# A hybrid decoder layer: weight slot views that start 8, 16 or 24 bytes further in or further back

## The chip, the core and the metric

The kernel runs on one core of one Trainium2 chip. The metric is the device time of one execution in microseconds (us), median of three runs.

## What is computed

One decoder layer over 256 tokens of width 1024, all in float32. The reference, cut to its products:

```python
h = rms_norm(x, attn_norm)
q_r, k_r, v_r, g_r, q_m, k_m, v_m = split(h @ w_in)        # 1024 x 6144
y_ret  = (group_norm(retention(rotary(q_r), rotary(k_r), v_r)) * silu(g_r)) @ w_ret_o
y_moba = attention(rms_norm(q_m), rms_norm(k_m), v_m) @ w_moba_o
gate_ret, gate_moba = split(sigmoid(h @ w_gate + b_gate))  # 1024 x 2048
x = x + (gate_ret * y_ret + gate_moba * y_moba) @ w_out
h = rms_norm(x, ffn_norm)
u_gate, u_val = split(causal_conv(h @ w_up))               # 1024 x 5632
x = x + (silu(u_gate) * u_val) @ w_down                    # 2816 x 1024
```

## The kernel before, in words

The weights are cut into 77 halves of 128 x 2048 float32 (1 MB each), numbered n = 0 to 76, and pass through four slots; half n uses slot r = n mod 4. A half is loaded by DMA into `w_raw{r}`. Then it is split in two: ScalarE (ACT) writes its high part, rounded to float32r, to the first 2048 elements of a view of `w_pair{r}` (line 635), and VectorE (DVE) writes the remainder, the low part, to the 2048 elements behind (line 912). Every product x @ w is three matmuls: high by high, high by low, low by high. The activations are split the same way, in `h_hi`, `h_lo`, `a_hi` and `a_lo`.

TensorE (PE) uses a half in one of two roles. A matmul has a stationary operand, 128 columns that are loaded before it (a weight load, PEld), and a moving operand that streams through.

- In **channel halves** the weights are the stationary operand and the activations move, 256 columns a matmul (`channel_half`, lines 377 to 379): 48 matmuls a half. There are 44 such halves: Q_R, K_R, G_R0, G_R1, GATE_R0, GATE_R1, RET_O0, RET_O1, GATE_M0, GATE_M1, MOBA_O0 and MOBA_O1 (n = 4 to 11 and 24 to 39), and n = 46 to 65 of the up-projection. Each slot has 11 of them.
- In **token halves** the activations are stationary and the weights move, 512 columns a matmul: 24 matmuls a half. These are V_R0, V_R1 (n = 0 to 3), Q_M0 to V_M1 (n = 12 to 23), all in `token_half`, lines 342 to 344; OUT0, OUT1 and UP0 (n = 40 to 45, `one_tile`, lines 530 to 532); and the down-projection (n = 66 to 76, lines 612 to 615). Without the down-projection these are 22 halves, five each in slots 2 and 3 and six each in slots 0 and 1.

`w_parts(n, r)` gives the two views of a slot. A slot is `SHIFT + 2 * HALF_ELEMS` elements long, `SHIFT` is 8 elements (32 bytes), so 32 bytes are spare. A view for moving weights starts 32 bytes in and a view for stationary weights at 0. The halves n = 66 and 67 (slots 2 and 3) are split inside a hardware loop whose views are those of stationary weights, so they start at 0 although their weights move.

Tensors stand one behind the other in SBUF, each rounded up to 32 bytes. In the built program `w_pair0` to `w_pair3` begin at bytes 110976, 127616, 144256 and 160896 of a partition, all multiples of 128; `h_hi`, `h_lo`, `a_hi` and `a_lo` begin at 49312, 57504, 65696 and 88224, all 32 past a multiple of 64.

ACT and DVE split half n as soon as half n - 4 has been used (`half_used`) and its data are there (`raw_loaded`); PE waits for `lo_ready` of the half that it begins. Between splits ACT and DVE read PSUM banks and do norms, softmax, gates and the convolution. The same engines also write and read `u_in`, rows of 258 elements whose data begin at the third element.

Of the kernel before, what the change touches and what calls it, by code (L numbers as in the profile page):

```python
# [20 lines left out]
SHIFT = 8  # L21
# [34 lines left out]
def hybrid_layer(nc, x, x_chan0, x_chan1, x_chan2, weights, gain_row_in, cols, ident_in, mask_in, rotary_in, decay_in, out):  # L56
# [8 lines left out]
    with ExitStack() as ctx:  # L65
# [154 lines left out]
        def w_parts(n, r=None):  # L220

            r = n % SLOTS if r is None else r
            if isinstance(n, int):
                moving = n // 2 in TOKEN_BLOCKS or n >= DOWN_FIRST_HALF + 2
            else:
                moving = False
            first = SHIFT if moving else 0
            return [w_pair[r][:, first + HALF_ELEMS * i:first + HALF_ELEMS * i + HALF_ELEMS] for i in range(2)]

        block = ctx.enter_context(nc.Block())  # L230
# [89 lines left out]
        def _(pe):  # L320
# [12 lines left out]
            def token_half(out_banks, n, tiles, first, last, before=None, src=(h_hi, h_lo)):  # L333

                hi, lo = (w.rearrange("p (k c) -> p k c", k=4) for w in w_parts(n))
                for kk, t in [(kk, t) for kk in range(4) for t in range(NT)]:
                    if before and t == 0:
                        before(kk)
                    k = tiles[kk]
                    s_hi, s_lo = (part[:, k, P * t:P * t + P] for part in src)  # L340
                    o = out_banks[t][:, :]
                    mm(o, s_hi, hi[:, kk, :], start=(first and kk == 0), stop=False)  # L342
                    mm(o, s_hi, lo[:, kk, :], start=False, stop=False)  # L343
                    ins = mm(o, s_lo, hi[:, kk, :], start=False, stop=(last and kk == 3))  # L344
                return ins
# [22 lines left out]
            def channel_half(banks, n, slot, r_hi, r_lo, h):  # L368

                hi, lo = (w.rearrange("p (k c) -> p k c", k=4) for w in w_parts(n, slot))  # L370
                for m in range(4):
                    o = banks[m // 2][:, SEQ * (m % 2):SEQ * (m % 2) + SEQ]
                    for kk in range(4):
                        k = 4 * h + kk
                        s_hi, s_lo = hi[:, kk, P * m:P * m + P], lo[:, kk, P * m:P * m + P]

                        mm(o, s_hi, r_hi[:, k, :], start=(k == 0 and m % 2 == 0), stop=False)  # L377
                        mm(o, s_hi, r_lo[:, k, :], start=False, stop=False)  # L378
                        ins = mm(o, s_lo, r_hi[:, k, :], start=False, stop=(k == KT - 1 and m % 2 == 1))  # L379
                return ins  # L380
# [23 lines left out]

            pe.wait_ge(zeros_ready, 1)
            zeros = w_parts(SLOTS - 1)[1][:, 0:512]
            def keep_warm(count):
                for _ in range(count):
# [895 lines left out]
```

## Time and profile before

| | |
|---|---|
| median of 3 runs | 471.55 us (471.36 to 471.68) |
| the profiled execution | 471.34 us, span 469.5 us |
| granted TensorE clock | 0.999 of full |
| PE, PEld, DVE, ACT busy | 99%, 91%, 64%, 54% of the span |
| weight halves through the slots | 77, of which 44 stationary, 33 moving |

The busy time of PE says that it always had a matmul under way. Matmuls overlap in such a profile, so their mean durations add up to more than the span; how fast they follow each other is read from the starts of two halves and the number of matmuls between them.

### The profile page before, as it was taken

The page shows a single profiled execution, that of the slowest core. Times are in us where ns is not written, and L with a number is a line of the kernel's source. Part 1 is how long each engine was busy: PE and PEld are TensorE (multiplying, and loading weights), DVE is VectorE, ACT ScalarE, POOL GpSimd, SP SyncE. Part 2 cuts the span into 40 slices and gives each one's busy share as a digit, 9 for nine tenths or more (in the row PEclk, how much of TensorE's full clock was granted, in tenths as well). Part 3 has the DMA queues.
Part 4 walks back from the last instruction along what each step waited for, and adds up shares of the span by engine and source line. Part 5 has one row for each costly group of instructions (what it writes and reads, how often), then busy time and mean ns, then how long its engine had stood idle before and what let it go on. Part 6 is the DMA issues. An engine that isn't in the chain of part 4 may idle for free.

```text
span 469.5 us, 7781 instructions
## 1 busy us (share of the span) xinstructions
PE 463.6 (99%) x3117; PEld 426.8 (91%) x3117; DVE 300.1 (64%) x364; ACT 254.5 (54%) x362; POOL 19.6 (4%) x27
## 2 busy tenths in 40 slices
PE   8999999999999999999999999999999999999997
PEld 5889999888888999999999788999999999988885
DVE  4797883764665547355338676688778888884312
ACT  5775432147774839334445355777777767663400
POOL 0210000311110001000000000000000000000000
PEclk9999999999999999999999999999999999999999
DMA  7997444254445523843453633616555555548002
GB/s 273 423 403 271 180 179 181 91 179 154 147 151 211 223 102 136 357 157 131 167 188 135 269 136 131 241 69 238 202 187 197 193 207 193 188 139 309 0 1 89
DMA packets 13978, 87.20 MB, mean 186 GB/s; under 512 B 1536, under 2 KB 1920, under 8 KB 4352
## 3 DMA queue, kind: packets, MB, share of 16 engines
q1 hardware_dynamic: 13536, 85.25, 48.6%
q0 software_dynamic: 416, 1.57, 0.9%
q8 instruction: 20, 0.33, 0.3%
q14 instruction: 6, 0.05, 0.0%
HBM read 85.77 MB, written 1.05 MB: 185 GB/s over the span
## 4 chain that ended last, share of the span: by engine, by line
PE 98%; DMA 1%; DVE 1%; ACT 0%; issue 0%
PE bank L377 18%; PE bank L379 18%; PE bank L378 17%; PE bank L342 6%; PE bank L343 6%; PE bank L344 6%; PE bank L612 4%; PE bank L615 4%; PE bank L613 4%; PE bank L530 2%; PE bank L532 2%; PE bank L531 2%; PE bank L396 2%; DMA w_raw<-weights_dram 1%; PE bank L462 1%; PE bank L480 1%
## 5 line engine op out<-in xcount | busy, mean ns | idle before, releaser
L912 DVE TENSOR_TENSOR w_pair<-w_raw,w_pair 128x2048 fp32r<-128x2048 f32 x75 | 170.4, 2288 | 78.1 <-ACT w_pair L635 77.9
L377 PE MATMUL bank<-h_hi,w_pair 128*128 128x256 f32 x576 | 161.7, 281 | 0.0
L378 PE MATMUL bank<-h_lo,w_pair 128*128 128x256 f32 x576 | 160.8, 279 | 0.0
L379 PE MATMUL bank<-h_hi,w_pair 128*128 128x256 f32 x576 | 160.7, 279 | 0.0
L635 ACT ACTIVATE w_pair<-w_raw 128x2048 fp32r<-128x2048 f32 x75 | 141.9, 1918 | 31.0 <-PE bank L615 17.1
L377 PEld LDWEIGHTS bank<-h_hi,w_pair 128*128 128x128 f32 x576 | 108.3, 188 | 0.4 <-issue 0.4
L378 PEld LDWEIGHTS bank<-h_lo,w_pair 128*128 128x128 f32 x576 | 108.3, 188 | 0.1
L379 PEld LDWEIGHTS bank<-h_hi,w_pair 128*128 128x128 f32 x576 | 108.3, 188 | 0.0
L1175 DVE SCALAR_TENSOR_TENSOR area<-area,col 128x256 f32<-128x256 f32 x88 | 37.8, 481 | 16.8 <-ACT area L838 14.2
L342 PE MATMUL bank<-w_pair,h_hi 128*128 128x512 f32 x96 | 37.9, 395 | 0.0
L344 PE MATMUL bank<-w_pair,h_lo 128*128 128x512 f32 x96 | 37.4, 390 | 0.0
L343 PE MATMUL bank<-w_pair,h_hi 128*128 128x512 f32 x96 | 37.4, 389 | 0.0
L377 PE MATMUL bank<-a_hi,w_pair 128*128 128x256 f32 x128 | 36.0, 281 | 0.0
L378 PE MATMUL bank<-a_lo,w_pair 128*128 128x256 f32 x128 | 35.8, 279 | 0.0
L379 PE MATMUL bank<-a_hi,w_pair 128*128 128x256 f32 x128 | 35.7, 279 | 0.0
L613 PE MATMUL bank<-w_pair,a_hi 128*128 128x512 f32 x88 | 34.4, 390 | 0.0
L612 PE MATMUL bank<-w_pair,a_hi 128*128 128x512 f32 x88 | 34.3, 390 | 0.0
L615 PE MATMUL bank<-w_pair,a_lo 128*128 128x512 f32 x88 | 27.9, 390 | 0.0
L378 PEld LDWEIGHTS bank<-a_lo,w_pair 128*128 128x128 f32 x128 | 24.1, 188 | 0.0
L379 PEld LDWEIGHTS bank<-a_hi,w_pair 128*128 128x128 f32 x128 | 24.1, 188 | 0.0
L377 PEld LDWEIGHTS bank<-a_hi,w_pair 128*128 128x128 f32 x128 | 24.0, 188 | 0.0
L834 ACT ACTIVATE area<-bank 128x512 f32<-128x512 f32 x20 | 12.0, 601 | 20.8 <-PE bank L379 20.8
(132 smaller groups left out, 563.8 us busy)
## 6 DMA issues: line engine op xcount, KB each, us to landing
w_raw<-weights_dram SPq DMA_DIRECT2D x75, 1024.0 KB, 4.8
w_raw<-weights_dram SPq DMA_DIRECT2D x3, 512.0 KB, 7.7
ys<-x_dram SPq DMA_DIRECT2D x2, 512.0 KB, 12.8
xs<-x_dram POOLq DMA_DIRECT2D x1, 1024.0 KB, 8.8
out_dram<-ys SPq DMA_DIRECT2D x4, 256.0 KB, 2.0
area<-decay_dram SPq DMA_DIRECT2D x1, 768.0 KB, 13.5
w_raw<-weights_dram SPq DMA_DIRECT2D x2, 256.0 KB, 4.1
xs<-x_chan_dram SPq DMA_DIRECT2D x1, 512.0 KB, 6.2
```

What stands on the lines that cost most here:

```text
L342: mm(o, s_hi, hi[:, kk, :], start=(first and kk == 0), stop=False)
L343: mm(o, s_hi, lo[:, kk, :], start=False, stop=False)
L344: ins = mm(o, s_lo, hi[:, kk, :], start=False, stop=(last and kk == 3))
L377: mm(o, s_hi, r_hi[:, k, :], start=(k == 0 and m % 2 == 0), stop=False)
L378: mm(o, s_hi, r_lo[:, k, :], start=False, stop=False)
L379: ins = mm(o, s_lo, r_hi[:, k, :], start=False, stop=(k == KT - 1 and m % 2 == 1))
L612: mm(bank[4 + 2 * t + c][:, :], s_hi, hi[:, kk, c, :], start=(k == 0), stop=False)
L613: mm(bank[4 + 2 * t + c][:, :], s_hi, lo[:, kk, c, :], start=False, stop=False)
L615: ins = mm(bank[4 + 2 * t + c][:, :], s_lo, hi[:, kk, c, :], start=False, stop=(k == D_FF // P - 1))
L635: A(w_parts(n, r)[0], raw[r][:, :], ACT.Copy).then_inc(hi_ready, 1)
L912: tt(lo, raw[r][:, :], hi.bitcast(f32), ALU.subtract).then_inc(lo_ready, 1)
L1175: ins = stt(out=conv[:, jj, m, :], in0=u_in[:, jj, m, tap:tap + SEQ], scalar=conv_col(4 * m + tap), in1=conv[:, jj, m, :], op0=ALU.mult, o ...
```

## The change

The start of a slot's view takes in the slot's number r. A view for stationary weights starts at 0, 8, 16 and 24 bytes in slots 0, 1, 2 and 3; one for moving weights at 32, 24, 16 and 8 bytes. Slot 0 is as before. All instructions, their order and their waits are the same on every engine; only these addresses differ. The raw slots, to which the DMAs write, and the activations stay where they are. The halves 66 and 67, whose weights move but are split in the loop, start at 16 and 24 bytes in place of 0.

```diff
-            first = SHIFT if moving else 0
+            first = SHIFT - 2 * r if moving else 2 * r
             return [w_pair[r][:, first + HALF_ELEMS * i:first + HALF_ELEMS * i + HALF_ELEMS] for i in range(2)]
```

## Rows read from the trace of the kernel before

**Rows 1.** The page: span and the busy time of each engine.

```profile
span 469.5 us, 7781 instructions
PE 463.6 (99%) x3117; PEld 426.8 (91%) x3117; DVE 300.1 (64%) x364; ACT 254.5 (54%) x362; POOL 19.6 (4%) x27
```

**Rows 2.** The chain that ended last, share of the span by engine.

```profile
PE 98%; DMA 1%; DVE 1%; ACT 0%; issue 0%
```

**Rows 3.** Matmul groups by line and shape: count, busy us, mean ns, idle before.

```profile
L377 PE MATMUL bank<-h_hi,w_pair 128*128 128x256 f32 x576 | 161.7, 281 | 0.0
...
L342 PE MATMUL bank<-w_pair,h_hi 128*128 128x512 f32 x96 | 37.9, 395 | 0.0
...
L377 PE MATMUL bank<-a_hi,w_pair 128*128 128x256 f32 x128 | 36.0, 281 | 0.0
...
L613 PE MATMUL bank<-w_pair,a_hi 128*128 128x512 f32 x88 | 34.4, 390 | 0.0
...
L530 PE MATMUL bank<-w_pair,h_hi 128*128 128x512 f32 x48 | 19.0, 395 | 0.0
...
L342 PE MATMUL bank<-w_pair,a_hi 128*128 128x512 f32 x32 | 13.7, 428 | 0.8 <-DVE a_lo L923 0.8
```

**Rows 4.** Windows of one half each (218.82: seven), first matmul to next half's first.

```profile
core 0: us, PE busy (x) PEld busy (x) DVE busy (x) ACT busy (x) POOL busy (x), PEclk, DMA share, GB/s
406.05:411.65 5.60, 5.60 (x27) 4.51 (x25) 3.96 (x10) 3.54 (x7) 0.00 (x0) 1.00 0.81 312
411.65:417.25 5.60, 5.60 (x26) 4.51 (x24) 3.78 (x4) 5.20 (x4) 0.00 (x0) 1.00 0.00 0
...
422.71:428.15 5.44, 5.44 (x25) 4.50 (x24) 3.01 (x2) 1.92 (x1) 0.00 (x0) 1.00 0.99 358
428.15:433.59 5.44, 5.44 (x25) 4.50 (x24) 2.29 (x1) 1.92 (x1) 0.00 (x0) 1.00 0.74 303
...
89.33:94.77 5.44, 5.44 (x25) 4.50 (x24) 5.11 (x9) 0.00 (x0) 0.29 (x1) 1.00 0.45 184
218.82:258.40 39.58, 39.58 (x338) 39.58 (x337) 20.29 (x14) 17.05 (x17) 0.00 (x0) 1.00 0.49 179
230.13:235.78 5.65, 5.65 (x51) 5.65 (x49) 2.44 (x2) 0.00 (x0) 0.00 (x0) 1.00 0.74 267
327.65:333.25 5.60, 5.60 (x50) 5.60 (x49) 3.75 (x9) 4.71 (x8) 0.00 (x0) 1.00 0.84 323
```

**Rows 5.** Timeline of PE: the first matmul of halves 52, 53, 66 and 67.

```profile
327.65 0.28 PE L377 MATMUL bank<-h_hi,w_pair 128*128 128x256 f32 x1
...
333.25 0.28 PE L377 MATMUL bank<-h_hi,w_pair 128*128 128x256 f32 x1
...
406.05 0.39 PE L612 MATMUL bank<-w_pair,a_hi 128*128 128x512 f32 x1
...
411.65 0.40 PE L612 MATMUL bank<-w_pair,a_hi 128*128 128x512 f32 x1
```

**Rows 6.** The chain in order of time: sixteen transposes of 128 columns.

```profile
105.82 1.75 PE bank L396 x16
```

**Rows 7.** Groups of ACT and DVE by line and shape.

```profile
L635 ACT ACTIVATE w_pair<-w_raw 128x2048 fp32r<-128x2048 f32 x75 | 141.9, 1918 | 31.0 <-PE bank L615 17.1 <-PE bank L379 10.7 <-PE bank L532 2.1
...
L1175 DVE SCALAR_TENSOR_TENSOR area<-area,col 128x256 f32<-128x256 f32 x88 | 37.8, 481 | 16.8 <-ACT area L838 14.2 <-DVE area L1175 0.6
...
L834 ACT ACTIVATE area<-bank 128x512 f32<-128x512 f32 x20 | 12.0, 601 | 20.8 <-PE bank L379 20.8
...
L923 DVE SCALAR_TENSOR_TENSOR a_lo<-xs,a_hi 128x256 fp32r<-128x256 f32 x8 | 3.8, 479 | 0.0
...
L663 ACT ACTIVATE area<-bank 128x512 f32<-128x512 f32 x4 | 2.2, 600 | 5.5 <-PE bank L344 5.5
```

**Rows 8.** Timeline of DVE and PE where half 43 is split and begun.

```profile
264.40 2.29 DVE L912 TENSOR_TENSOR w_pair<-w_raw,w_pair 128x2048 fp32r<-128x2048 f32 x1 [1.12 <-ACT w_pair L635]
...
266.84 0.41 PE L530 MATMUL bank<-w_pair,h_hi 128*128 128x512 f32 x1
```

## The prediction

> **What bounds the kernel now.** I read the page first: PE is busy in 99% of the 469.5 us, with full clock, and DVE and ACT in 64% and 54% [rows 1]. The chain of work that ended last is PE for 98% [rows 2]. So the time is that of a stream of matmuls, and the only question is how far apart two of them start. Their groups give the counts [rows 3]: 3 x (576 + 128) = 2112 matmuls with stationary weights (256 columns), and 3 x (96 + 32 + 48 + 88) = 792 with moving weights (512 columns).
>
> The distance comes from windows that reach from one half's first matmul to the next half's [rows 4]; how such an edge is found is seen in the timeline [rows 5]. A channel half of 48 matmuls takes 5.60 us: 116.7 ns each. A token half of 24 takes 5.44 us: 226.7 ns each. In the channel window the weight loads (PEld) are busy for the whole 5.60 us; in the token window for 4.50 of 5.44 us [rows 4]. So loads have no slack in channel halves, and have some in token halves. Transposes, which also load 128 columns each, start 1.75/16 = 109 ns apart [rows 6]; a channel matmul is 7.3 ns over that.
>
> Two rows show that addresses count. Halves 66 and 67 move weights from offset 0 and take 5.60 us each; halves 69 and 70 do the same work from offset 32 and take 5.44 us [rows 4]. The difference is 0.16 us a half, 6.7 ns a matmul (3%). It isn't the DMA: half 67 has a DMA share of 0.00 and half 69 one of 0.99. And half 35, a channel half with the same addresses as others, takes 5.65 us against 5.60 [rows 4]: the same reads cost 1.0 ns a matmul more when load and stream stand differently to each other in time, and seven halves in a row, 33 to 39, do so: 39.58 us, 5.65 each [rows 4].
>
> **The change part by part.** No instruction, wait or DMA is added, removed or moved. What is left is the price of an address, for four kinds of access.
>
> *Moving reads.* Touched are the token halves of slots 1 to 3 outside 66 and 67: 16 halves of the first kinds (V, Q_M to V_M, OUT, UP0: six in slot 1, five each in slots 2 and 3), and six of the down-projection (69 to 71 and 73 to 75). They go from offset 32 to 24, 16 and 8. The bounds are the two ends in the rows: at 32 bytes 5.44 us, at 0 bytes 5.60 us. In between I take a straight line, 0.04 us a half for each 8 bytes: slot 1 has 8 halves at 0.04, slot 2 has 7 at 0.08, slot 3 has 7 at 0.12, together 0.32 + 0.56 + 0.84 = +1.72 us. If anything but 32 costs the whole step, it is 22 x 0.16 = +3.5 us; if nothing below a whole 32 bytes costs, 0. Halves 66 and 67 go the other way, from 0 to 16 and 24: -0.08 - 0.12 = -0.20 us (bounds 0 and -0.32). The sum is +1.5 us.
>
> *Stationary reads.* 33 channel halves, 11 in each of slots 1 to 3, load their weights from 8, 16 or 24 bytes in, while the activations still move from 32 past a multiple of 64. The trace has no load at such an address, so this is the unknown. From below: a channel matmul can't start faster than the 109 ns of a transpose, so the gain is at most 33 x 48 x 7.3 ns = 11.6 us. From above I take the moving step of 6.7 ns for each load: 33 x 48 x 6.7 ns = +10.6 us. Zero lies inside. The nearest row is the one with the same instructions and another position of load to stream: half 35 at 5.65 us, +0.05 us a half. Shifting the load's addresses by 8 to 24 bytes does that to them, so I take that price. Of the 33 halves, six (33, 34, 35, 37, 38, 39) pay it already: 27 x 0.05 = +1.35 us.
>
> The Trainium skill (SBUF — State Buffer, Specifications) gives SBUF 16-byte cachelines with a penalty for each cross to a new line. It speaks against this change in slots 1 and 3; it is a rival below. The same skill (TensorE: Matmul & The Clock Gate, Part 2, step by step) says that TensorE has two independent read ports and that loading the next weights doesn't take read bandwidth from the running matmul. By it the stationary term would be 0 and the sum +1.5 us; I don't rely on it, since its isolated gap of N/2.4 + 2.5 ns would be 215.8 ns for 512 columns and the trace has 226.7.
>
> *Writes of ACT and reads of DVE in the slots.* ACT writes its results to u_in at 8, 16, 24 and 32 bytes past a multiple of 64 in 601 ns (L834), and to an aligned tile in 600 ns (L663) [rows 7]. DVE reads the same rows 0 and 4 bytes before that in 481 ns (L1175) and aligned operands in 479 ns (L923) [rows 7]. No row has DVE writing off 16 bytes; from below that is 0, from above I take the moving step of 3% on the 2.29 us of a split, 0.07 us. I take 0 for all of it. What hides it: a split pair takes 1.92 us + 2.29 us [rows 7, 8] and PE spends 5.4 us or more in a half. The thinnest cover found is at half 43: its split ends at 264.40 + 2.29 = 266.69 us and PE begins it at 266.84 [rows 8]. That leaves 0.15 us, more than 0.07. With the cover gone there, the cost would be the 0.07 us of that one half, since later splits catch up while PE works on the halves in hand.
>
> *The sum.* 1.52 + 1.35 = +2.9 us on the profiled execution's own 471.34 us: 474.2. The median of the runs is 0.2 us above that execution, so I give 474.4 us.
>
> **The rivals.**
>
> *Loads lose a whole step.* Loads have no slack in channel halves (PEld 5.60 of 5.60), so one fetch more for a load that starts off its natural boundary goes straight to the end. For it: 33 halves are touched, and this stage is two thirds of the matmul time. Against it: nothing in the trace shows such a load. At 6.7 ns it gives 1.5 + 10.6 = +12.1 us, 483.7; at half of that per load +6.8 us, 478.4. Chance 0.20, most of it nearer the lower value.
>
> *Nothing under 32 bytes counts.* The reader fetches in large pieces and has the start early enough; only 0 against 32 is seen. Then moving views off 0 stay at the cheap rate and loads don't change, and 66 and 67 gain at most 0.32: 471.2 to 471.6. For it: ACT and DVE show no price for 8 bytes. Against it: they move far less in a nanosecond than this stream, and two offsets of 32 bytes already differ. Chance 0.20. (If instead all offsets under 32 are treated as 0, that is +3.5 - 0 us, 475.1; it is counted with the forecast.)
>
> *Lines of 16 bytes.* One more line for a view that starts in the middle of one: slots 1 and 3 pay, slot 2 pays nothing. Priced from the rows as one part in 128 of 226.7 ns for a stream of 2048 bytes, 1.8 ns, and one in 32 of 116.7 ns for a load of 512 bytes, 3.6 ns: 15 token halves x 24 x 1.8 ns = 0.6 us, and 22 channel halves x 48 x 3.6 ns = 3.8 us: +4.4 us, 476.0. Chance 0.08. This is the penalty of the SBUF page of the Trainium skill.
>
> *Faster: the new start takes loads and stream out of each other's way.* A channel matmul has 7.3 ns over the transposes' distance, and a token matmul of offset 0 shows 6.7 ns of such a loss that another offset takes away. If shifted loads meet the stream less and win half of it, 33 x 48 x 3.6 ns = 5.8 us, against +1.5 for the moving part: -4.3 us, 467.3. It decides from 0.05 us a channel half (1.0 ns a matmul) on: then 33 x 0.05 = 1.6 us outweigh the moving term. Against it: it needs a better position than the present one in most slots at once. Chance 0.14.
>
> **How the numbers follow.** The forecast (moving views priced by bytes or as 0, loads little) has 0.38, with its own range 472.6 to 476.8. The range leaves out the faster case but for its edge, and the upper part of the loads' case: 470.7 to 481.5. A measurement of this kernel can tell about 0.2%, 0.94 us, from no change. Faster by more: 0.13. Within it: 0.20, the second rival and the weakest forms of others. Slower: 0.67.
>
> **What would show it.** In the profile after, the token halves should be 5.44 us in slot 0, near 5.48 in slot 1, 5.52 in slot 2 and 5.56 in slot 3, halves 66 and 67 near 5.52 and 5.48. Equal times in slots 1 to 3 at 5.60 would mean rounding down; an excess in slots 1 and 3 alone would mean lines of 16 bytes. Channel halves of slots 1 to 3 should be 5.60 to 5.70 us, those of slot 0 5.60 or, where a neighbour leaves its position behind, 5.65. Channel halves of 5.9 us or 5.4 us would prove the forecast wrong at its unknown. ACT L635 and DVE L912 should keep 1918 ns and 2.29 us, and PE should wait for them nowhere new.

## The result and the profile after

The changed kernel takes 478.31 us (477.93 to 478.64) beside 471.47 us for the kernel before on the same chip: a ratio of 1.0146 [1.0133, 1.0158], 6.8 us slower. The profiled execution took 478.64 us. The page of the changed kernel, first its span and busy times, then its chain by engine, then its groups (count, busy us, mean ns of one, idle before it):

```profile
span 476.8 us, 7781 instructions
...
PE 469.8 (99%) x3117; PEld 429.7 (90%) x3117; DVE 300.3 (63%) x364; ACT 254.8 (53%) x362; POOL 19.6 (4%) x27
...
PE 95%; DMA 2%; DVE 1%; SPq 1%; ACT 1%; issue 0%
...
L912 DVE TENSOR_TENSOR w_pair<-w_raw,w_pair 128x2048 fp32r<-128x2048 f32 x75 | 170.5, 2289 | 80.6 <-ACT w_pair L635 80.4
L377 PE MATMUL bank<-h_hi,w_pair 128*128 128x256 f32 x576 | 162.7, 282 | 0.0
...
L635 ACT ACTIVATE w_pair<-w_raw 128x2048 fp32r<-128x2048 f32 x75 | 141.9, 1919 | 32.1 <-PE bank L615 17.7
```

The kernel is bound as before [rows 1, 2]: PE is busy in 99% of a span that is 7.3 us longer. Its idle time is 476.8 - 469.8 = 7.0 us against 5.9; the 1.1 us more lie in the opening halves, which wait for their data, except for 0.02 us. They cost nothing: half 2 starts at 19.24 us where it started at 19.61, and half 4 at 31.16 after 31.17. This is also why PE has 95% of the chain in place of 98%: the chain now reaches half 2 through the load and the split of its weights. Matmul records overlap, so I go by starts below. ACT's split takes 1919 ns after 1918, DVE's 2289 ns after 2.29 us [rows 7, 8]. So the time is lost between the starts of matmuls. Windows of one half each, from its first matmul to the next half's first. In order: halves 52 to 55 (channel, slots 0 to 3), half 14 (token, slot 2), halves 66, 67 (slots 2, 3, loop views), and 69 to 71 (slots 1 to 3):

```profile
core 0: us, PE busy (x) PEld busy (x) DVE busy (x) ACT busy (x) POOL busy (x), PEclk, DMA share, GB/s
332.06:337.72 5.66, 5.66 (x50) 5.66 (x49) 3.68 (x9) 4.78 (x8) 0.00 (x0) 1.00 0.79 316
337.72:343.63 5.91, 5.91 (x50) 5.91 (x49) 5.70 (x4) 3.02 (x3) 0.00 (x0) 1.00 0.28 90
343.63:349.26 5.63, 5.63 (x50) 5.63 (x49) 3.37 (x8) 4.63 (x8) 0.00 (x0) 1.00 0.71 279
349.26:354.91 5.65, 5.65 (x51) 5.65 (x49) 5.53 (x5) 3.17 (x3) 0.00 (x0) 1.00 0.23 51
95.70:101.37 5.67, 5.67 (x26) 4.57 (x25) 2.13 (x2) 5.47 (x18) 1.84 (x2) 1.00 0.47 185
412.18:417.85 5.67, 5.67 (x26) 4.57 (x25) 3.81 (x9) 3.55 (x7) 0.00 (x0) 1.00 0.67 277
417.85:423.45 5.60, 5.60 (x25) 4.53 (x24) 3.78 (x4) 5.25 (x4) 0.00 (x0) 1.00 0.00 0
...
428.94:434.54 5.60, 5.60 (x25) 4.52 (x24) 2.93 (x2) 1.93 (x1) 0.00 (x0) 1.00 1.00 369
434.54:440.14 5.60, 5.60 (x25) 4.50 (x24) 2.29 (x1) 1.92 (x1) 0.00 (x0) 1.00 0.65 263
440.14:445.77 5.63, 5.63 (x25) 4.56 (x24) 2.29 (x1) 1.92 (x1) 0.00 (x0) 1.00 0.00 0
```

Beside [rows 4]: half 53 took 5.60 us and takes 5.91; halves 54 and 55 take 5.63 and 5.65; half 52, whose address hasn't changed, went from 5.60 to 5.66. The down halves in slots 1 to 3 took 5.44 and take 5.60 to 5.63. The clock is 1.00 in each. The next table adds the differences of such windows between the two profiles over all halves, each stretch counted for the half whose matmuls begin it (worked out from the starts of matmuls):

```
us, after - before    slot 0   slot 1   slot 2   slot 3   sum
channel halves         0.39     2.80     0.32     0.38    3.9
token halves           0.14     1.04     1.02     1.13    3.3
66, 67; n = 0 to 3; ahead of the first matmul: 0.07, -0.14, 0.13
```

The first four halves (n = 0 to 3) begin with waits for data, so their dearer matmuls (some 236 ns a matmul in slot 2) cost nothing. The rest makes up the 7.3 us. 2.8 us of it lie in slot 1's channel halves alone: in 9 of the 11 the matmuls start 123.3 ns apart, in the other two (n = 25 and 29) 117.8 ns, from the same addresses.

### The profile page after: what moved, and what is told of

Read it like the earlier page. It is cut to its first block, busy times and chain, and to the rows that moved or that the text cites. A ratio compares the mean times of both kernels' runs of the same rounds, so it can differ in the third digit from the quotient of the medians.

```text
span 476.8 us, 7781 instructions
## 1 busy us (share of the span) xinstructions
PE 469.8 (99%) x3117; PEld 429.7 (90%) x3117; DVE 300.3 (63%) x364; ACT 254.8 (53%) x362; POOL 19.6 (4%) x27
## 4 chain that ended last, share of the span: by engine, by line
PE 95%; DMA 2%; DVE 1%; SPq 1%; ACT 1%; issue 0%
PE bank L377 18%; PE bank L379 18%; PE bank L378 18%; PE bank L342 6%; PE bank L344 5%; PE bank L343 5%; PE bank L612 4%; PE bank L613 4%; PE bank L615 4%; PE bank L530 2%; PE bank L531 2%; PE bank L532 2%; DMA w_raw<-weights_dram 2%; PE bank L396 2%; PE bank L462 1%; PE bank L480 1%
## 5 line engine op out<-in xcount | busy, mean ns | idle before, releaser
L912 DVE TENSOR_TENSOR w_pair<-w_raw,w_pair 128x2048 fp32r<-128x2048 f32 x75 | 170.5, 2289 | 80.6 <-ACT w_pair L635 80.4
L635 ACT ACTIVATE w_pair<-w_raw 128x2048 fp32r<-128x2048 f32 x75 | 141.9, 1919 | 32.1 <-PE bank L615 17.7
L342 PE MATMUL bank<-w_pair,h_hi 128*128 128x512 f32 x96 | 38.5, 401 | 0.0
L343 PE MATMUL bank<-w_pair,h_hi 128*128 128x512 f32 x96 | 37.9, 395 | 0.0
```

Of the source, the lines that this page charges most:

```text
L635: A(w_parts(n, r)[0], raw[r][:, :], ACT.Copy).then_inc(hi_ready, 1)
L912: tt(lo, raw[r][:, :], hi.bitcast(f32), ALU.subtract).then_inc(lo_ready, 1)
```

## The experiments

"Load" is the weight load of the stationary operand, "stream" the reads of the moving one. Times are medians against the kernel before on the same chip.

### The two parts apart, and which offset

```diff
-            first = SHIFT if moving else 0
+            first = SHIFT - 2 * r if moving else 0         # e1_moving_alone
+            first = SHIFT if moving else 2 * r             # e2_stationary_alone
```

> Only the views of moving weights are shifted (24, 16, 8 bytes in slots 1, 2, 3); stationary views start at 0 as before. If the two parts of the change add up, as the trace of the changed kernel says (token halves there take 5.58 to 5.67 us in slots 1 to 3 against 5.44), this part alone costs some +3.5 to 4 us: 475.0 to 475.5 us, with channel halves back at 5.60. Rival: the loss in channel halves is set off by the state in which a shifted token half leaves the stream; then channel halves of slot 1 stay near 5.9 us here too, and the kernel takes near 478.

> Only the views of stationary weights are shifted (8, 16, 24 bytes in slots 1, 2, 3); moving views start at 32 as before, and halves 66 and 67 move from 16 and 24. If the parts add up: +3 to 3.5 us, 474.5 to 475 us, nearly all of it in channel halves of slot 1, whose matmuls are 123 ns apart as in the changed kernel, 117 to 118 in slots 0, 2 and 3. Rival: a price for each load that starts off its 16-byte line: then slot 3 (24 bytes) would pay as slot 1 (8 bytes) does; the trace of the changed kernel already speaks against it (117.6 ns).

The moving part alone: 474.83 against 471.39 us, 1.0076 [1.0059, 1.0093], +3.4 us. The stationary part alone: 475.05 us, 1.0079 [1.0062, 1.0096], +3.7 us. The sum is 7.1 against 6.8 measured for both, so the parts add up. Windows of the first (half 53, slot 1; half 14, slot 2):

```profile
335.51:341.11 5.60, 5.60 (x50) 5.60 (x49) 5.49 (x4) 3.08 (x3) 0.00 (x0) 1.00 0.20 57
95.02:100.68 5.66, 5.66 (x25) 4.57 (x24) 2.10 (x2) 5.46 (x18) 1.84 (x2) 1.00 0.58 185
```

And of the second (half 52, slot 0; half 53, slot 1; half 14):

```profile
329.46:335.12 5.66, 5.66 (x50) 5.66 (x49) 3.68 (x9) 4.78 (x8) 0.00 (x0) 1.00 0.78 316
335.12:341.04 5.92, 5.92 (x51) 5.92 (x50) 5.70 (x4) 3.02 (x3) 0.00 (x0) 1.00 0.28 90
95.01:100.45 5.44, 5.44 (x26) 4.50 (x24) 2.04 (x2) 5.24 (x18) 1.84 (x2) 1.00 0.52 193
```

In these windows each role pays where its own addresses moved, with one exception: slot 0 pays 0.06 us a half though nothing of it moved. Other halves show the same thing. With only the moving views shifted, no address of a channel half has changed, yet halves 5 to 8 go from 5.60 to 5.65 us and halves 33 to 39 from 5.65 to 5.60; over all channel halves that adds up to nothing. With only the stationary views shifted, 7 of the 11 halves of slot 1 are at 5.91 us, and halves 5 and 9, which were among the dear ones in the changed kernel, run at 117.8 ns a matmul.

Then the same four offsets in another order, and one offset in all slots:

```diff
-            first = SHIFT if moving else 0
+            first = SHIFT if moving else (0, 6, 2, 4)[r]   # e4_rotated
+            first = SHIFT if moving else 4                 # e12_stationary_16
```

> Stationary views start at 0, 24, 8 and 16 bytes in slots 0, 1, 2, 3 (before the change 0 in all, in the changed kernel 0, 8, 16, 24); moving views as before at 32. If the offset of 8 bytes is what costs, the matmuls 123 ns apart go to the channel halves of slot 2, slots 1 and 3 have 117 to 118, and the time is that of the stationary part alone, 474.5 to 475.5 us. Rival: slot 1 is dear for its place in the pipeline or in memory, or because it follows slot 0: then slot 1 stays at 123 ns or a half that follows slot 0 does, whatever its offset.

> All stationary views at 16 in all four slots, moving ones at 32 as before. The offset 16 cost 0.5 ns a matmul in slot 2 of the changed kernel (117.2), but the sweeps and the pairs give 120.0 for it where it keeps its own position. With no other offset in between, all channel halves should hold it: 120.0 ns, 5.76 us a half, 44 x 0.15 = +6.6 us: 478 us, as much as the whole change for an offset that looked cheap there. Rival: an offset has its own price, whatever stands in the other slots: then 44 x 48 x 0.5 = +1.1 us, 472.6 us.

Rotated: 473.22 against 471.61 us, 1.0031 [1.0019, 1.0043], +1.6 us, where the unrotated order cost +3.7. Its windows of halves 49 (24 bytes), 50 (8 bytes), 51 (16 bytes) and 55 (16 bytes again):

```profile
312.07:317.71 5.64, 5.64 (x50) 5.64 (x49) 5.50 (x7) 4.15 (x3) 0.00 (x0) 1.00 0.10 12
317.71:323.36 5.65, 5.65 (x50) 5.65 (x49) 4.59 (x9) 4.65 (x8) 0.00 (x0) 1.00 0.91 358
323.36:328.99 5.63, 5.63 (x51) 5.63 (x49) 5.51 (x5) 3.14 (x3) 0.00 (x0) 1.00 0.19 61
345.94:351.69 5.75, 5.75 (x50) 5.75 (x49) 5.63 (x5) 3.14 (x3) 0.00 (x0) 1.00 0.23 66
```

8 bytes cost 5.65 us here and 5.91 in the changed kernel; 16 bytes cost 5.63 or 5.75 in one and the same slot. So an offset has no single price. All slots at 16 bytes: 475.80 against 471.55 us, 1.0086 [1.0071, 1.0102], +4.3 us, and again both values, here for halves 34 and 51:

```profile
226.34:231.97 5.63, 5.63 (x50) 5.63 (x49) 2.02 (x1) 5.18 (x6) 0.00 (x0) 1.00 0.10 41
324.51:330.27 5.76, 5.76 (x50) 5.76 (x49) 5.70 (x4) 3.02 (x3) 0.00 (x0) 1.00 0.26 77
```

Expectations that gave an offset or a slot a price missed in both, and so did the one that 16 bytes hold 120.0 ns in every half: halves 33 to 39 are at 117.2 to 117.4 ns.

### What a half inherits from the one before

Groups of 48 matmuls (24 of 512 columns) appended to the kernel before, in pairs, with a plain float32 transpose ahead of each pair; no ACT or DVE work beside them.

```python
apart()     # one plain transpose of the identity
for j in range(48): mm(bank[0][:, 0:256], S(0, j), M(32, j, 256), start=True, stop=True)
for j in range(48): mm(bank[0][:, 0:256], S(8, j), M(32, j, 256), start=True, stop=True)
...
apart()
for j in range(48): mm(bank[0][:, 0:256], S(16, j), M(32, j, 256), start=True, stop=True)
for j in range(48): mm(bank[0][:, 0:256], S(8, j), M(32, j, 256), start=True, stop=True)
```

> The kernel before with 32 pairs of groups behind its last product, each pair opened by a plain transpose: 48 matmuls of 256 columns with load offset p, then 48 with load offset n (stream at 32); and 24 matmuls of 512 columns with stream offset p, then 24 with n (load at 32). If the distance is a function of the two addresses alone, the second group of a pair depends on n and not on p. If load and stream lock into one of several positions and keep it, the same n gives several distances, according to p: n = 8 near 117.8 behind the transpose and near 123 behind p = 0, as the changed kernel has it behind slot 0.

One run, 834.17 us. Windows from the first to the last start of a group (47 distances): load at 8 behind a load at 0, at 8 behind 16, at 16 behind 8, at 16 behind 16.

```profile
483.13:488.67 5.54, 5.54 (x50) 5.54 (x49) 0.00 (x0) 0.00 (x0) 0.00 (x0) 1.00 0.01 3
575.19:580.98 5.79, 5.79 (x49) 5.79 (x48) 0.00 (x0) 0.00 (x0) 0.00 (x0) 1.00 0.01 3
540.72:546.23 5.51, 5.51 (x49) 5.51 (x48) 0.00 (x0) 0.00 (x0) 0.00 (x0) 1.00 0.00 0
587.07:592.71 5.64, 5.64 (x49) 5.64 (x48) 0.00 (x0) 0.00 (x0) 0.00 (x0) 1.00 0.01 3
```

Divided by 47 these are 117.9, 123.2, 117.2 and 120.0 ns: the values of the kernels within 0.1 ns, without ACT and DVE. So a pair of addresses can have more than one lasting rate, and what ran before decides which it runs at. Which predecessor does it was not as I had guessed for offset 8: behind 0 it runs at 117.9 here, where slot 1 of the changed kernel, behind slot 0 at offset 0, runs at 123.3. A transpose in between doesn't wipe this out either: of four groups at 16 right behind one, two run at 117.4 ns and two at 119.9 (second half of each group).

In the kernel itself: the change, and one plain float32 matmul of 128 columns (of zeros) ahead of each channel half from n = 24 on.

```diff
+            def plain(o, h):
 ...
+                mm(o, mask[:, 0:P], ident[:, :], start=(h == 0), stop=(h == 0))
 ...
+                if apart:
+                    plain(banks[0][:, 0:P], h)
```

> The changed kernel with one plain matmul of 128 columns, of zeros, added in front of each channel half from 24 on (36 of the 44). If slot 1's 123.2 ns are a position handed on by the slot-0 half before it, the plain matmul takes it away: halves 33, 37, 49, 53, 57, 61, 65 go from 5.91 to 5.66 us, and the time gains 7 x 0.26 = 1.8 us less 36 x 0.15 us for the added matmuls, 5.4: some 482 us. If offset 8 costs this by its address, they stay at 5.91 us plus the added matmul, 484 us. The sign is in the halves, not in the total.

484.52 against 471.49 us, 1.0280 [1.0263, 1.0297]. Half 49, slot 1, offset 8, with the added matmul in the window:

```profile
318.44:324.31 5.87, 5.87 (x53) 5.87 (x52) 5.76 (x5) 3.36 (x3) 0.00 (x0) 1.00 0.21 50
```

The added matmul, with a slow start of the ones behind it, costs 0.23 us a half (5.85 against 5.62 us in a kernel further down whose rate it leaves alone, `e14_acts16_w32_apart` against `e10_acts16_w32`), so the 48 matmuls of this half take 5.64 us, 117.5 ns each, not 123.3. Behind that start, ten of the eleven halves of slot 1 are at 117.7 to 118.0 ns; half 9, which has no plain matmul ahead of it, stays at 123.3. So the offset alone doesn't make slot 1 dear: 0.27 us of its 0.31 us a half depend on what ran before. Half 5, at the same addresses and without a plain matmul too, runs at 117.8 ns in this execution and at 123.3 in the changed kernel's, though PE has the same instructions and addresses ahead of it. The time missed the expected 482 us, since the added matmul was taken as 0.15 us: 36 x 0.23 us less 7 x 0.27 us for the halves named there is 6.4 us on 478.3, or 484.7. Slot 2 lost by it: 6 of its 9 halves behind a plain matmul run at 120.0 ns, the others at 117.4, where the changed kernel has 117.3 in nearly all. So the plain matmul changes the rate that a half takes; it neither sets one rate nor is it a cure.

### The pair of addresses

64 pairs of load offset S and stream offset M (8 byte steps) appended to the kernel before, one tile pattern, a transpose ahead of each.

> The kernel before with 128 groups of float32r matmuls behind its last product, one line each: 48 matmuls of 256 columns or 24 of 512, for each pair of a load address S and a stream address M, both 0 to 56 bytes past a multiple of 64 in steps of 8; one plain transpose keeps groups apart, and no other engine works. Theory 1, each operand pays for its own start: the distance of matmuls is a sum of a term of S and a term of M, so rows of the table differ from each other by a constant. Theory 2, load and stream meet in the memory: the distance depends on S and M together, with the dear pairs along diagonals, S minus M or S minus half of M constant, and differs from the kernel's own numbers little: (S 0, M 32) 116.7 ns and (S 8, M 32) 123 ns at 256 columns, (S 32, M 32) 226.7 and (S 32, M 0) 233.3 at 512. Theory 3, it needs the traffic of ACT and DVE on the same memory: then all pairs are alike here and near 109 and 216 ns.

One run, 1219.77 us. At 256 columns, with M = 32: 116.6 ns at S = 0, 117.8 at 8, 120.1 at 16, 117.6 at 24, each a value that halves of the kernels show too; lowest 113.3 at (S 8, M 48) and (S 40, M 16) (means over the second half of each group, without its slow beginning). Every stream that starts off 16 bytes (M = 8, 24, 40, 56) is at 118.9 or more, whatever the load. At 512 columns the low pairs reach 226.6 and a stream off 16 bytes never does (230.2 to 240.0). So both things are there: a price of the stream's own start, and one of how load and stream stand to each other. The traffic of ACT and DVE isn't needed for either.

Kernels that should use the low pairs (activations at `ACT_AT`, views at `STATIONARY_AT` and `MOVING_AT`, in elements; small tensors moved so that every slot starts alike):

```diff
-SHIFT = 8
+STATIONARY_AT, MOVING_AT = 10, 4     # e6_acts16_w40_16, ACT_AT = 12; e7_acts48_w8_48: 2, 12, ACT_AT = 4
 ...
-            first = SHIFT if moving else 0
+            first = MOVING_AT if moving else STATIONARY_AT
```

> The sweep says where load and stream disturb each other least: at 256 columns with the stream at 16 and the load at 40 bytes past a multiple of 64 (113.8 ns), at 512 with both at 16 (226.7). So all activations start 16 past a multiple of 64, stationary weights 40 and moving weights 16, the same in all slots; small tensors between the slots are moved behind them to make room. If the distance in the kernel is set by these two addresses, channel matmuls fall from 116.9 to about 113.8 ns, 2112 x 3.1 = 6.5 us, and the kernel takes some 465 us. Rival: the sweep's low cells are positions that hold only behind a transpose; in the kernel each half starts in the position that the half before leaves, and channel halves stay at 117 ns or more: 471 us or above.

> As the kernel with activations at 16, stationary weights at 40 and moving weights at 16, but all of them 32 bytes further on (48, 8, 48 past a multiple of 64). If only the position of load to stream counts, and the stream's place in its 16-byte and 32-byte pieces, this takes the same time as that kernel within 1 us. If the place within 64 bytes counts for itself, as the sweep has it for 512 columns (load and stream at 48: 231.1 ns, at 16: 226.7), the token halves are 4 ns a matmul dearer: 792 x 4.4 = +3.5 us against that kernel.

Both missed: 478.94 and 480.31 against 471.61 us, 1.0155 [1.0141, 1.0169] and 1.0185 [1.0170, 1.0201]. The second is 1.4 us above the first, between the two cases expected for it (within 1 us, and 3.5 us more). Channel halves went to 120.0 ns, except halves 28 to 31 at 115.5 to 117.8; one of the first kernel:

```profile
315.04:320.80 5.76, 5.76 (x51) 5.76 (x50) 5.65 (x6) 3.94 (x3) 0.00 (x0) 1.00 0.17 26
```

In both, the high and the low part of the activations had come to stand 64 bytes apart modulo 128, which the sweep (modulo 64) didn't see. That, put into the kernel before (16 more elements ahead of `h_lo` and `a_lo`):

> The kernel before with one thing moved: the low parts of the activations, h_lo and a_lo, begin 96 instead of 32 bytes past a multiple of 128 (the high parts stay at 32, all stay 32 past a multiple of 64). The two kernels with activations at 16 and at 48 had high and low parts 64 apart modulo 128 as well, and their channel matmuls were 120.0 ns apart where the sweep, whose operands all kept one place modulo 128, had 113.8. If bytes count modulo 128, channel matmuls go to some 119 to 120 ns here too, 2112 x 3 = +6 us, 477 to 478 us. If only the place modulo 64 counts, this is the kernel before: 471.5 us within 0.5.

476.44 against 471.50 us, 1.0108 [1.0091, 1.0125], +4.9 us, a little under the expected 477 to 478; channel halves of the up-projection 5.65 us (117.7 ns), less than expected, and token halves at 231 to 233 ns. The spare elements make `h_lo` 128 bytes longer, so `a_hi` stands 128 bytes further on too, which is another place modulo 256. The halves that use `h_hi` and `h_lo` don't have this, and they lose 3.2 of the 4.9 us. So 64 bytes count. The sweep again with the kernel's own order of high and low parts and modulo 128:

> The sweep again, with the kernel's own order of three products (high by high, high by low, low by high) and all places modulo 128: loads in steps of 8, streams in steps of 16, each group opened by a plain transpose; 48 matmuls of 256 columns, 24 of 512. If places count modulo 128 and only the distance from load to stream matters besides, cells with stream minus load = 40 at 256 columns are near 113.5 wherever the stream starts 16 past a multiple of 32, and the kernel's own pair (load 0, stream 32) is at 116.7. If each address counts for itself, the low cells are single ones: (8, 48) and (40, 80) and no shifts of them.

One run, 1963.53 us. Two windows, from first to last start: (load 0, stream 32), as in the kernel before, and (load 40, stream 80).

```profile
656.15:661.72 5.57, 5.57 (x50) 5.57 (x49) 0.00 (x0) 0.00 (x0) 0.00 (x0) 1.00 0.00 0
968.37:973.82 5.45, 5.45 (x51) 5.45 (x50) 0.00 (x0) 0.00 (x0) 0.00 (x0) 1.00 0.01 3
```

Part of the table (ns between starts, 256 columns, mean over the second half of each group, so without its slow beginning):

```
stream \ load   0      8      16     24     32     40     104
16            118.7  117.8  120.0  120.0  113.3  120.0  113.3
32            116.7  117.8  120.0  117.8  120.0  115.5  118.3
48            118.3  113.3  118.3  120.0  118.7  120.0  119.3
80            120.0  118.3  118.3  118.8  118.3  113.3  118.3
```

Loads at 8, 40, 72 and 104 with the stream 40 bytes further (modulo 128) all give 113.3. The distance isn't all: at 40 bytes with the stream on a multiple of 32 (loads at 24, 56 and 88) it is 120.0. Two kernels built on it, both with all activations in one tensor so that high and low stand alike:

> Chosen from the second sweep: all activations start 16 past a multiple of 128, all weight views 32, stationary or moving (and so halves 66 and 67 too); the activations stand in one tensor, so that high and low parts keep one place. The sweep has (load 32, stream 16) at 113.3 ns for 256 columns and (load 16, stream 32) at 226.7 for 512. If the two places modulo 128 set the distance, channel matmuls go from 116.9 to 113.4 ns, 2112 x 3.5 = -7.4 us, halves 66 and 67 save 0.3: 463.8 us. Rival: the position that the sweep found holds only behind a plain transpose and the kernel's halves fall into others; then channel matmuls are at 117 to 120 ns and the time is 471 us or more.

> The kernel that was meant with activations at 16, stationary weights at 40, moving weights at 16, now with high and low parts of the activations at one place modulo 128 (80). The sweep has 113.3 ns for (load 40, stream 80) and for its three shifts by 32, and 226.7 for two of the three shifts that stand for (load 80, stream 16). If the places modulo 128 were what went wrong in that kernel (120.0 ns), this one has 113.3 ns in channel halves and takes 464 to 464.5 us; if something else did, it takes 471 us or more.

Both missed again: 472.62 and 474.21 against 471.55 us, 1.0024 [1.0015, 1.0033] and 1.0059 [1.0045, 1.0073]. A channel half of the first and one of the second, 117.1 and 118.3 ns a matmul where the table has 113.3:

```profile
323.17:328.79 5.62, 5.62 (x51) 5.62 (x49) 5.50 (x5) 3.17 (x3) 0.00 (x0) 1.00 0.21 55
```

```profile
323.71:329.39 5.68, 5.68 (x50) 5.68 (x49) 5.56 (x5) 3.13 (x3) 0.00 (x0) 1.00 0.22 71
```

### Why the low pairs didn't carry over

Three rivals: inherited position (the first kernel with a plain matmul ahead of each channel half), the order of tiles (groups in the kernel's order, behind others), and the form of the matmuls (`h_hi` in place of `a_hi`, adding up in PSUM, outputs spread over banks, four tiles).

> The same plain matmul in front of each channel half from 24 on, in the kernel with activations at 16 and all weights at 32. If its channel matmuls are at 117.1 ns in place of the sweep's 113.3 because a half inherits the position of the one before, they go to 113.3 behind the plain matmul: 36 x 48 x 3.8 = -6.6 us, + 5.4 for the added ones: 471.5 us. If the kernel's order of tiles does it, they stay at 117.1 and the time is 478 us.

> Behind the kernel before, groups of 36 matmuls of 256 columns with the kernel's own order of tiles within a half (512 bytes from column block to column block, 2048 from tile to tile), for eight pairs of load and stream place: three times the same behind a plain transpose, and then every pair behind every other. If positions are handed on, a group's distance depends on the group before it and stays the same through three groups of one pair; offset (8, 32) is at 117.8 by itself and at 123.3 behind some other. If the order of tiles matters, the pairs (32, 16) and (40, 80), 113.3 in the sweep, are at 117.1 and 118.3 here already right behind the transpose.

> Groups of 36 matmuls of 256 columns (48 with four tiles), three times the same behind a plain transpose, for the pairs (0, 32), (32, 16), (8, 48), (40, 80), each in seven forms: as in the sweep; with h_hi and h_lo as streams; adding up in PSUM; with outputs spread over halves of two banks as in the kernel; and these together, up to the kernel's own form. The form in which (32, 16) leaves 113.3 ns for some 117 names what the sweep left out. If none does, the difference lies in the work of the other engines, which only the kernel has.

480.15 against 471.49 us, 1.0188 [1.0171, 1.0205]: behind the slow start that follows the plain matmul, channel halves stay at 117.1 ns, so it isn't inherited. In the other two (one run each, 1119.38 and 820.57 us) the pairs (32, 16), (40, 80) and (8, 48) run at 113.3 in the kernel's order, behind every other pair, and in every form tried (four tiles not with (40, 80)), and (0, 32) at 116.5 to 117.9. All three rivals fall. The first of the two shows more than one rate again, for (16, 32) 117.1 to 117.5 or 119.8 to 120.2 and for (96, 32) 113.3 or 117.8, both also right behind a transpose; but (8, 32) stays at 117.6 to 118.4 behind all eight, so the 123.3 ns that were expected behind one of them didn't come. What was left for the kernels was the distance between the tensors: in the sweeps the stream starts 112 and 40 bytes further on than the load modulo 256 for these two pairs, in the two kernels 240 and 168, 128 more. The last two kernels test that: the same offsets, activations and order of instructions, once at distance 40 modulo 256, once with a spare tensor of 128 bytes ahead of the slots.

```diff
+STATIONARY_AT, MOVING_AT = 2, 16
+SPARE = 16
+ACT_AT = 12
 ...
+            first = MOVING_AT if moving else STATIONARY_AT
 ... and in e18_slots128_on alone:
+        between = sb("between", [P, 32])
         w_pair0 = sb("w_pair0", [P, SPARE + 2 * HALF_ELEMS], f32r)
```

> Slots begin 128 past a multiple of 256 as before, stationary weights 8 bytes in, moving weights 64 in, all activations 176 past a multiple of 256. Stream minus load is then 40 in channel halves (the sweep: 113.3 ns at all four places 16 past a multiple of 32) and 16 in token halves (226.7). If the distance counts modulo 256, channel matmuls are at 113.3 ns: 2112 x 3.6 = -7.6 us, some 464 us. If it is something that the sweeps don't have (other engines' work), they are at 116 to 120 ns again and the time is 471 us or more.

> The kernel of the run before with a spare tensor of 128 bytes in front of the slots: every distance from load to stream is the same modulo 128 and another modulo 256. If it counts modulo 256, channel matmuls leave 113.3 ns for 117 to 120 as in the kernels built before (118.3 for distance 168), and the time is 473 to 475 us. If it counts modulo 128, both runs are alike within 0.5 us.

464.92 against 471.42 us, 0.9866 [0.9851, 0.9881]: 6.5 us faster than the kernel before, 13.4 faster than the changed one. With the spare 128 bytes 478.73 us, 1.0156 [1.0143, 1.0170]: channel matmuls at 118.3 ns as expected, but the time missed 473 to 475 us, since the stationary activations of the token halves stand elsewhere to their streams too and those matmuls went from 226.7 to 233.3 ns. Half 51 of each, 113.3 and 118.3 ns a channel matmul:

```profile
317.82:323.26 5.44, 5.44 (x50) 5.44 (x49) 5.32 (x5) 3.38 (x3) 0.00 (x0) 1.00 0.36 102
```

```profile
326.64:332.32 5.68, 5.68 (x50) 5.68 (x49) 5.56 (x5) 3.12 (x3) 0.00 (x0) 1.00 0.24 68
```

ACT and DVE have the same instructions in both (3 and 5), the clock is 1.00, and the dearer one has the lower DMA share (0.24 against 0.36); only the addresses tell the two apart. (In these two, `ss_x` and `inv_x` also stand elsewhere than in the kernel before.)

## Why the prediction was right and wrong

**Right: the bound and the sign.** A stream of matmuls was the whole kernel before and is after; behind the opening halves no wait took its place (0.02 us in all; at half 43, the thinnest cover, the split ends at 267.77 + 2.29 = 270.06 us and PE begins at 270.30); ACT and DVE kept 1919 and 2289 ns; DMA has no part (half 67 costs 5.60 us with a DMA share of 0.00, half 69 5.60 us with 1.00). Two starting addresses that differ by 32 bytes were rightly read as a warning for the streams.

**Wrong: the moving term, +1.5 us.** The step that failed is the straight line between the prices at 32 and at 0 bytes. Alone, this part costs +3.4 us. Streams from 24, 16 and 8 bytes cost 232.6, 236.0 and 236.0 ns in Q_M halves where 0 bytes costs 233.3: nearly the whole step or more at once, near the upper bound of +3.5. Halves 66 and 67 were to gain 0.2 us and gained nothing (5.67 and 5.60 against 5.60). There is a price for a start off 16 bytes (the sweep: never under 230.2 ns at 512 columns), but 16 bytes, a multiple, is dear too; it also changes how the stream stands to the load, which by the sweep sets the price with it.

**Wrong: the stationary term, +1.35 us.** Alone, this part costs +3.7 us. The failed step is that half 35's 5.65 us, one position of one pair of addresses, was taken as the price of any offset. Slots 2 and 3 came out near it (5.63, 5.65), as did slot 0, which the text had allowed "where a neighbour leaves its position behind". Slot 1 at 5.91 us did what the prediction had said would prove it wrong: +2.8 us in that slot. It isn't 8 bytes as such (5.65 us rotated), nor slot 1 (5.64 rotated), nor ACT and DVE (123.2 ns without them). It is the rate that a half at 8 bytes keeps from what ran before it: 117.8 or 123.3 ns. The reason was mentioned for slot 0 and not priced for the others. One reading behind both this term and the first rival doesn't hold: PEld busy for the whole 5.60 us was taken to mean that loads have no slack. In the fastest kernel a channel half takes 5.44 us with PEld busy for all of it, so a full PEld row doesn't say that loads set the distance.

**The rivals.** Loads that lose a whole step gave 478.4 at half a step per load, and the measured time is there, but by other means: 3.7 us from the loads and 3.4 from the streams, not 5.3 and 1.5. That the total agrees is luck. "Nothing under 32 bytes counts" falls with both single parts. "Lines of 16 bytes" falls: it had slot 2 free, and slot 2's streams, at 16 bytes, cost as much as any. The sweep agrees with part of it: a stream that starts off 16 bytes pays at every load. "Faster" had a sound mechanism, a better position of load to stream: 113.3 ns exists, 3.4 ns under the kernel's, and gave 6.5 us once found. These four offsets just don't hit it. By the Trainium skill (TensorE: Matmul & The Clock Gate, Part 2, step by step) a load takes no read bandwidth from the running matmul. The load's address would then cost nothing. In the sweep it alone moves the distance from 115.6 to 120.1 ns with the stream held at 32, so for this stream of float32r matmuls the measurement goes against the rule.

**Open.** Why distances count modulo 256 (or a larger power: more than 256 wasn't tried), which unit of the memory is behind it, and by what rule a group picks between its two rates. The runs show that the pair of addresses and what ran before set the rate; they don't show a reason inside the memory. Token halves of the fastest kernel stay near 228.3 ns instead of 226.7 in part, unexplained.

## What to carry to other kernels

In this back-to-back stream of float32r matmuls with a load each, where loads and streams stand to each other modulo 256 bytes is worth 3% (464.92 against 478.73 us for one spare tensor of 128 bytes), so an edit of buffers can move the time though no instruction changes; look for it with windows from one tile's first matmul to the next tile's. Price such an address by a sweep of pairs in the kernel's own order and with the tensors' true distances, not by a line between two rows; a row that shows two rates for equal addresses (here 5.60 and 5.65 us) says that the neighbour counts too. In such a stream, don't start a moving operand off 16 bytes (118.9 ns or more in the sweep, where the best is 113.3).

## What the hardware showed that I had not expected

- Only the cheapest pairs run evenly: 113.3 ns at 256 columns is 113, 113, 114 over and over, and 226.7 at 512 is 226, 227, 227. At 2.4 GHz, the level at which all of this ran (granted clock 1.00), these are 272 and 544 cycles. The dearer means are repeating patterns: 116.7 is 116, 117, 120, 114; 120.0 is 122, 118; 123.3 is 122, 125.
- A rate, once taken, lasts for the whole of a half, and equal addresses hold two of them: 117.8 and 123.3 ns (8 bytes), 117.3 and 120.0 ns (16 bytes).
- Moving the low part of the activations by 64 bytes modulo 128 costs 4.9 us, 3.2 of them where nothing else of the operands moved modulo 256.
- A plain float32 matmul of 128 columns between float32r matmuls costs 0.23 us, twice the distance of 256-column float32r matmuls; some 0.09 us of it is that the matmuls behind it start a little further apart at first (119.0 ns on average over the half, 117.1 in its second half).
